# A mixture of experts on one core: norm, routing and first gathers in one stage, job lists from one-hot products, the combine joined to the experts

## The reference, cut to what matters

```python
def hmoe(xn, w_rg, b_rg, w_re, b_re, w_gate, w_up, w_down):
    ...
    lg = (x @ w_rg + b_rg).astype(F32)
    g_sel = jnp.argmax(lg, axis=-1)
    p_g = jnp.max(jax.nn.softmax(lg, axis=-1), axis=-1)
    le = (x @ w_re + b_re).astype(F32).reshape(-1, N_GROUPS, EXPERTS_PER_GROUP)
    le_g = jnp.take_along_axis(le, g_sel[:, None, None], axis=1)[:, 0]
    top_p, top_i = lax.top_k(jax.nn.softmax(le_g, axis=-1), TOP_K_IN_GROUP)
    w_top = p_g[:, None] * top_p / jnp.sum(top_p, axis=-1, keepdims=True)
    ...
        hid = jax.nn.silu(jnp.einsum('nd,edf->nef', x, w_gate[gi])) * jnp.einsum('nd,edf->nef', x, w_up[gi])
        y = y + jnp.einsum('nef,ne,efd->nd', hid, c, w_down[gi]).astype(F32)

def run_group(x, past_len, wkv0, shift0, past_rows, win_buf, P):
    ...
        h = h + y
        h = h + hmoe(rmsnorm(h, P['ln_ffn'][layer]), *moe)
```

## Time and profile before

| | |
|---|---|
| median of 3 runs | 2490.96 us (2485.36 to 2492.52) |
| profiled execution | 2487.45 us, of which span 2485.8 us |
| busy: PE, PEld | 2110.0 us (85%), 1368.9 us (55%) |
| busy: DVE, ACT, POOL | 900.7 us (36%), 487.0 us (20%), 462.1 us (19%) |
| granted TensorE clock, mean | 0.915 |
| bytes moved by DMA | 409.74 MB, mean 165 GB/s |

### The profile page before, as it was taken

One profiled execution on the slowest core, in us unless ns is written; L12 is line 12 of the kernel. 1 busy time (PEld: TensorE's weight loads), 2 busy tenths in 40 slices (PEclk: granted clock), 3 DMA queues, 4 the chain that ended last, 5 costly groups with the idle time before them and its releaser, 6 DMA issues. The chain is left out here.

```text
span 2485.8 us, 44144 instructions
## 1 busy us (share of the span) xinstructions
PE 2110.0 (85%) x17339; PEld 1368.9 (55%) x17339; DVE 900.7 (36%) x1763; ACT 487.0 (20%) x1120; POOL 462.1 (19%) x548
## 2 busy tenths in 40 slices
PE   3899989998953999957987888799999975799993
PEld 2678789994752333326876555455555565233333
DVE  4655247743122111224133666434363022112123
ACT  1311112221011111101001555433343000111100
POOL 0144022220003233320002333000000001323322
PEclk7999999997865999978998999999999895899996
DMA  1498340001252999922440100555547416599952
GB/s 56 144 294 272 113 164 4 6 36 42 68 175 88 374 374 396 373 91 60 112 132 23 32 1 2 177 185 161 184 144 238 148 22 240 215 374 372 394 205 103
DMA packets 238894, 409.74 MB, mean 165 GB/s; under 512 B 56770, under 2 KB 194595, under 8 KB 212436
## 3 DMA queue, kind: packets, MB, share of 16 engines
q1 hardware_dynamic: 191140, 346.48, 38.8%
q0 software_dynamic: 40288, 56.12, 7.3%
q10 hardware_dynamic: 7264, 4.36, 0.6%
HBM read 499.03 MB, written 81.57 MB: 234 GB/s over the span
## 5 line engine op out<-in xcount | busy, mean ns | idle before, releaser
L1619 PE MATMUL banks<-slots,work 128*64 128x512 f32 x1536 | 342.6, 599 | 0.0
L2592 PE MATMUL banks<-slots 128*128 128x508 f32 x512 | 249.2, 601 | 8.7 <-ACT work L2692 7.3
L1619 PEld LDWEIGHTS banks<-slots,work 128*64 128x64 f32 x1536 | 106.2, 138 | 202.7 <-issue 201.8
L909 PE MATMUL banks<-slots 64*64 64x64 f32 x5632 | 188.9, 224 | 23.7 <-issue 7.2
L909 PEld LDWEIGHTS banks<-slots 64*64 64x64 f32 x5632 | 185.1, 140 | 25.8 <-issue 13.9
L671 PE MATMUL banks<-slots,work 128*128 128x260 f32 x768 | 175.3, 387 | 4.6 <-DMA z_state<-in_consts 4.6
L1645 PE MATMUL banks<-slots,work 128*64 128x512 f32 x768 | 175.3, 598 | 3.6 <-DVE work L1697 3.6
L2663 DVE COPY slots<-banks 64x256 f32<-64x256 f32 x256 | 109.2, 426 | 166.8 <-PE banks L2498 162.5
L1891 PE MATMUL banks<-slots,work 128*128 128x260 f32 x640 | 150.0, 397 | 18.0 <-PEq L251 16.2
L671 PEld LDWEIGHTS banks<-slots,work 128*128 128x128 f32 x768 | 145.9, 192 | 32.7 <-issue 6.2
L1331 POOL DMA_INDIRECT expert_lists<-work x20 | 19.6, 981 | 770.0 <-DVEq L251 764.5
(11 more groups left out here) (416 smaller groups left out, 3012.5 us busy)
## 6 DMA issues: line engine op xcount, KB each, us to landing
slots<-in_moe_wgate SPq DMA_DIRECT2D x64, 1024.0 KB, 9.1
slots<-in_moe_wup SPq DMA_DIRECT2D x64, 1024.0 KB, 11.6
slots<-in_moe_wdown SPq DMA_DIRECT2D x64, 1024.0 KB, 11.3
sample_cache_rows<-in_cache_kv POOLq DMA_DIRECT2D x128, 256.0 KB, 4.5
slots<-in_cache_kv SPq DMA_DIRECT2D x256, 128.0 KB, 2.2
slots<-sample_cache_rows SPq DMA_DIRECT2D x32, 512.0 KB, 6.5
slots<-sample_cache_rows SPq DMA_DIRECT2D x64, 256.0 KB, 5.0
slots<-expert_result_rows SPq DMA_DIRECT2D x8, 1024.0 KB, 9.1
```

The costliest lines, as they stand in the source:

```text
L909: last = nc.tensor.matmul(out[half, k, :], block_of(i, u, left)[half, k, :], moving[half, :], start=(x == 0), stop=(x == len(terms) - 1))
L1619: last = mm(c.bank[v][SEAT * j:SEAT * j + SEAT, :], xt[v][:, k, SEAT * j:SEAT * j + SEAT], weights.gate_up_of[2 * s + j][:, k], start=(k = ...
L2592: last = mm(HIDDEN[:, 0:KVH * NCMP_S], s.w1[:, u // NB, j, :], s.xt[u % 2][:, :, j % 8, first:first + NCMP_S], start=(j == 0), stop=(j == 15))
```

## The change

The norm becomes part of the routing stage, so that its loads and the weight loads are issued when the norm begins, and the eight tables become one load. The router's weights become the stationary side: the logits come as 36 rows of 520 columns, the bias is added on VectorE, and five transposes make the token tiles of them. The counts of both kinds come from six matmuls. The lists no longer pass through DRAM: VectorE spreads each entry over 24 columns (which pair) and a one-hot row of 128 (which seat), and ten matmuls add the entries up in PSUM as the lists. The first two fetches stand at the end of this stage. The clears of the fetch buffers move to POOL. The combine becomes the end of the experts stage: SP waits for the scatters, and VectorE makes the sums that POOL made.

```diff
 def route(c, layer, weights):
+    wr = area(KT, NL)
+    both_and_none, place, spill = area(NTILE + 1, E), area(NTILE, E), area(NTILE, E)
+    reached = area(NTILE, PAIRS + 1)
...
         @block.sync
         def _(sp):
+            sp.dma_start(table, io["consts"][:, lo:hi]).then_inc(loaded, 16)
             sp.dma_start(wr[:, :, 0:NG], io["moe_wrg"][layer].rearrange("(k p) n -> p k n", p=P)).then_inc(loaded, 16)
...
-            for dst, name in ((rank4, "rank4"), (rank8, "rank8"), (valid, "valid"), (token, "token"),
-                              (before, "triangle"), (seats, "seats"), (over_id, "overid")):
-                sp.dma_start(dst, io["consts"][:, CCOL[name][0]:CCOL[name][1]]).then_inc(loaded, 16)
...
         @block.gpsimd
         def _(pool):
-            pool.wait_ge(placed, 1)
-            pool.wait_ge(blank_stored, 16)
+            for v in range(2):
+                last = nc.gpsimd.memset(weights.tokens_in[v], 0.0)
+            last.then_inc(cleared, 1)
+            pool.wait_ge(cleared, 1)
+            pool.wait_ge(fetchable, 1)
+            pool.wait_ge(stored, 32)
+            for q in range(2):
+                weights.fetch(q)
+
+        @block.tensor
+        def _(pe):
...
+            pe.wait_ge(loaded, 16 * 5)
+            for k in range(KT):
+                pe.wait_ge(scaled, k + 1)
+                for s in range(2):
+                    last = mm(c.pair[1][0:NL, s, :], wr[:, k, :], x[:, k, span(s)], start=(k == 0), stop=(k == KT - 1))
+            last.then_inc(logits_in, 1)
+            pe.wait_ge(biased, 1)
...
             pe.wait_ge(chosen, 1)
+            mm(c.bank[1][:, 0:E * (NTILE + 1)], before, both_and_none.rearrange("p n e -> p (n e)"), start=True, stop=False)
+            for m in range(NTILE):
+                last = mm(c.bank[1][:, E * (m + 1):E * (NTILE + 1)].rearrange("p (n e) -> p n e", e=E), c.ones,
+                          both[:, m:m + 1, :].to_broadcast([P, NTILE - m, E]), start=False, stop=(m == NTILE - 1))
             last.then_inc(counted, 1)
+            for a in range(2):
+                pe.wait_ge(spread, a + 1)
+                for n in range(NTILE):
+                    last = mm(c.bank[2][:, 0:4 * PAIRS], seat_hot[:, a, n, :], entries[:, a, n].rearrange("p w q -> p (w q)"),
+                              start=(a == 0 and n == 0), stop=(a == 1 and n == NTILE - 1))
+            last.then_inc(listed, 1)
...
         @block.vector
         def _(dve):
+            dve.wait_ge(loaded, 16 * 5)
+            ts(limits, over_id[:, 0:MORE], float(SEAT), float(SEAT), ALU.mult, ALU.add)
+            ts(absent, valid, -FAR, FAR, ALU.mult, ALU.add)
+            dve.wait_ge(summed, 1)
+            ts(halves(root), c.pair[0], 1.0 / D, EPS, ALU.mult, ALU.add).then_inc(means, 1)
...
+            for k in range(KT):
+                nc.vector.scalar_tensor_tensor(x[:, k, :], h[:, k, :], c.vec(f"ffn{layer}", k), rstd, ALU.mult,
+                                               ALU.mult).then_inc(scaled, 1)
+            dve.wait_ge(logits_in, 1)
+            ts(halves(logits_t), c.pair[1][0:NL], bias[0:NL], None, ALU.add).then_inc(biased, 1)
...
+            for a, w in ((0, w1), (1, e2)):
+                tt(both, place, hot[a], ALU.mult)
+                dve.drain()
+                reduce(row[:, a, :].unsqueeze(2), both, AX.X, ALU.add)
+                dve.drain()
+                tt(row[:, a, :], row[:, a, :], absent[:, :, 0], ALU.add)
+                dve.drain()
+                tt(reached, row[:, a, :].unsqueeze(2).to_broadcast([P, NTILE, PAIRS + 1]),
+                   pair_start.unsqueeze(1).to_broadcast([P, NTILE, PAIRS + 1]), ALU.is_ge)
+                dve.drain()
+                reduce(first[:, a, :].unsqueeze(2), reached, AX.X, ALU.add)
+                there = entries[:, a, :, 3, :]
+                tt(there, reached[:, :, 0:PAIRS], reached[:, :, 1:PAIRS + 1], ALU.subtract)
...
+                tt(seat_hot[:, a], lane.unsqueeze(1).to_broadcast([P, NTILE, P]),
+                   seat[:, a, :].unsqueeze(2).to_broadcast([P, NTILE, P]), ALU.is_equal)
+                dve.drain().then_inc(spread, 1)
...
+            dve.wait_ge(listed, 1)
+            out = c.bank[2][:, 0:4 * PAIRS].rearrange("p (w q) -> p w q", w=4)
+            ts(empty, out[:, 3], -FAR, FAR + 0.25, ALU.mult, ALU.add)
+            nc.vector.tensor_copy(c.job_lists[:, :, 2].bitcast(F32), out[:, 2])
+            dve.drain()
+            for w in range(2):
+                tt(c.job_lists[:, :, w], out[:, w], empty, ALU.add)
+            dve.drain().then_inc(fetchable, 1)

 def experts(c, layer, weights):
...
+            sp.wait_ge(finished, PAIRS - 1)
+            for v in range(2):
+                sp.wait_ge(scattered[v], 16 * PAIRS // 2)
+            for n in range(NTILE):
+                m = P if n < TT else NB
+                two = c.expert_rows[2 * P * n:2 * P * n + 2 * m].rearrange("(p a) e -> p a e", a=2)
+                sp.dma_start(pairs[0:m, n], two).then_inc(rows_loaded[n], 16)
...
-            for v in range(2):
-                pool.wait_ge(scattered[v], 16 * PAIRS // 2)
...
+            def sum_rows(n):
+                m = P if n < TT else NB
+                dve.wait_ge(rows_loaded[n], 16)
+                nc.vector.tensor_tensor(pairs[0:m, n, 0, :], pairs[0:m, n, 0, :], pairs[0:m, n, 1, :],
+                                        ALU.add).then_inc(summed, 1)
+
+            sum_rows(0)
             for n in range(NTILE):
...
+                if n + 1 < NTILE:
+                    sum_rows(n + 1)
+                dve.wait_ge(sums_turned, n + 1)
...
 def mixture(c, layer):
-    rms_norm(c, c.slot(0), [(f"ffn{layer}", c.slot(1))], c.slot(3))
     weights = ExpertWeights(c, layer)
     route(c, layer, weights)
     experts(c, layer, weights)
-    combine(c, layer)
```

More of the change, by code:

```diff
@@ L1286, in route @@
     hot = [area(NTILE, E) for _ in range(2)]
-    both, place, spill = area(NTILE, E), area(NTILE, E), area(NTILE, E)
-    valid, token, before = area(NTILE, 1), area(NTILE, 1), area(P)
+    both_and_none, place, spill = area(NTILE + 1, E), area(NTILE, E), area(NTILE, E)
+    both = both_and_none[:, 0:NTILE, :]
     count, jobs_of, start, hop = area(E), area(E), area(E), area(E)
-    ones, seats, over_id = area(E), area(E), area(OVER)
+    ones = area(E)
     limits, past, owner, beyond = area(MORE), area(E, MORE), area(OVER), area(OVER)
@@ L1292, in route @@
     cube = area(OVER, E)
[L1293 to L1298, removed]
+    absent, row, seat, first = area(NTILE, 1), area(2, NTILE), area(2, NTILE), area(2, NTILE)
+    reached = area(NTILE, PAIRS + 1)
+    entries = area(2 * NTILE * 4 * PAIRS).rearrange("p (a n w q) -> p a n w q", a=2, n=NTILE, w=4)
+    seat_hot = c.flat(1, 3)[:, 10560:10560 + 2 * NTILE * P].rearrange("p (a n s) -> p a n s", a=2, n=NTILE)
@@ L1480, in _ @@
                ALU.is_gt)
+            ts(spill, place, float(SEAT), None, ALU.is_ge)
+            tt(place, place, seats.unsqueeze(1).to_broadcast([P, NTILE, E]), ALU.add)
             dve.drain()
@@ new lines, in _ @@
+                there = entries[:, a, :, 3, :]
+                tt(there, reached[:, :, 0:PAIRS], reached[:, :, 1:PAIRS + 1], ALU.subtract)
+                dve.drain()
+                ts(first[:, a, :], first[:, a, :], -float(P), float(P), ALU.mult, ALU.add)
+                tt(entries[:, a, :, 0, :], there, token.to_broadcast([P, NTILE, PAIRS]), ALU.mult)
+                tt(entries[:, a, :, 2, :], there, w.to_broadcast([P, NTILE, PAIRS]), ALU.mult)
+                dve.drain()
+                tt(seat[:, a, :], row[:, a, :], first[:, a, :], ALU.add)
@@ L1648, in _ @@
                 last.then_inc(finished, 1)
+            for n in range(NTILE):
+                m = P if n < TT else NB
+                pe.wait_ge(summed, n + 1)
+                if n >= 2:
+                    pe.wait_ge(added, 2 * (n - 1))
+                for k in range(KT):
+                    last = tr(c.bank[2 * (n % 2) + k // 4][:, P * (k % 4):P * (k % 4) + m],
+                              pairs[0:m, n, 0, P * k:P * k + P], c.ident[0:m, 0:m])
+                last.then_inc(sums_turned, 1)
         @block.scalar
```

243 lines of the change are left out of this document (100 added, 143 removed).

## The result

The changed kernel takes 2391.58 us (median of 4 runs, 2385.08 to 2394.02) against 2491.61 us (median of 4), a ratio of 0.9591 with a 95% interval of 0.9572 to 0.9610. The forecast was 2392. The profiled execution took 2392.51 us, its span 2390.9.

The account below looks back on a forecast made before the run. It took the mixtures' two ends, where one engine works and others wait (some 258 us), as the place to gain: 40.5 + 38.4 + 17.4 = 96.3 from 2487.45 gives 2391.2, forecast 2392 us, range 2381 to 2411.

Parts of the forecast that it names:

- Logits' copy, T0+24.4: Front: logits copied 24.4 us after the squares start (T0), before at T0+48.1; 23.7 us gained in layer 0.
- the two bounds (6.7 and 13.4): Logits' matmuls in the front: 6.7 us at full clock, 13.4 at half clock; 8.9 was taken.
- Copy to first fetch, 29.8: Front: counting and listing put the first token fetch 29.8 us after the logits' copy, bounds 27.5 and 33.
- Stage's end, T0+59.4: Routing stage's end: TensorE turns the first tokens 59.4 us after the squares start; gain 40.5 and 38.4 us.
- two cases: Routing stage's end: TensorE starts at T0+58.6 on the first fetch's landing, or about T0+60.3 if the second's is awaited.
- one of my signs of being wrong: Front: engines wait on POOL for over 4 us between the second fetch and TensorE's first turn of tokens.
- The other three signs: Means wait for a load; logits take over 11 us; combine's loads still start 10 us after the last scatter.
- POOL's end at 0.08 us per DMA: Stage ends: POOL's end grows by about 0.08 us per DMA issued, so two DMAs cost little.
- the rival of a long end at any count: Routing stage's end: POOL's end costs 8.4 us after landing however few its DMAs; 2409 us in all; 12%.
- the rival of the scatter's own completion: Experts' end: the 8.4 us are the scatter's completion, so SP waits as long; 16 us lost, 2408; 8%.
- Tail, 8.7 per layer: Last scatter to next norm: loads start 8.2 us earlier and sums save 0.5, 17.4 us in both layers.
- Sum, 96.3: Total gain: fronts 40.5 and 38.4 us plus tails 17.4, taken from the profiled 2487.45 us.

Follow-up runs that it names:

- the second execution: The changed kernel profiled again without any edit; median 2395.29 us, ratio 0.9608 to the kernel before.
- The two experiments: Changed kernel, one edit each: logits as before with tokens stationary, 2410.64 us; router and expert weight loads issued only once tokens are scaled, 2412.27 us.
- the run without it: Changed kernel with the routing and experts' stages closed without POOL's drain of its DMAs; median 2388.89 us, ratio 0.9597.

## Why the prediction was right, by its steps

**Logits' copy, T0+24.4:** 25.0 and 25.3, and 23.6 twice in the second execution. The matmuls took 9.9 and 10.1 us in the first execution and 8.5 in the second, against 8.9 taken, inside the two bounds (6.7 and 13.4): in layer 0 the granted clock was 0.72 over them in the first and 0.84 in the second. The loads released VectorE 4.0 us after T0, half of what I allowed, without effect. The two experiments give the shares of this step: each of the two edits, taken back alone, returns about 8 us of the 23. The other 7 were not divided further.

**Copy to first fetch, 29.8:** 29.4 and 29.4. Counts came at 13.3, as said. This is the listing without DRAM; its 18 us of gain (47.4 before) stand in the trace and were not tried apart; the place of the fetches ahead of the stage's end was not either.

**Stage's end, T0+59.4:** this was a middle of two cases, and the later was the true one (60.3; measured 60.2 and 60.4). The end waits for the second fetch, 1.5 and 1.6 us by the run without it. By the letter one of my signs of being wrong came up, a wait of over 4 us between second fetch and first turn (4.35 and 4.27); but nearly all of it is that fetch's own landing, which I had priced, and not a long end. The other three signs stayed away.

**POOL's end at 0.08 us per DMA:** taken out, the end gives back 1.63 us at 19 DMAs and 7.9 at 96, and with it in, the way grows at the same price up to 118. The fall beyond that, three readings below 100 could not show. With 2 DMAs it hides under the landing, so the rival of a long end at any count fell, and the rival of the scatter's own completion with it (2.55 us without the end).

**Tail, 8.7 per layer:** 10.3 and 9.4. Loads at 2.2 (2.3 taken) give 8.3 in both layers. The sum on VectorE took 1.23 us (1.25 taken). By the Trainium skill, "VectorE: DVE Perf Modes", section on the TRN2 errata, the estimate was 1.22, and the row agrees. From the first arrival to the end of the last add it took 13.2 and 13.4 (13.4 taken). The term that was off in layer 0 is the first arrival: 4.8 us after the loads' issue, where I kept 6.1. That 6.1 was a reading of layer 0 alone. Timeline of layer 1 in the kernel before:

```profile
2434.69 2.46 SPq L1725 DMA_DIRECT2D slots<-expert_result_rows  x5
2439.48 4.83 POOL L1744 TENSOR_TENSOR slots<-slots 128x1024 f32<-128x1024 f32 x2 [14.28 <-DMA slots<-expert_result_rows]
```

There the first data came 4.79 us after the issue already, so the arrival gives 1.3 us in layer 0 and nothing in layer 1. The two late arrivals on record, 6.07 in the kernel before and 6.37 in the same without POOL's end, are both in layer 0 and go with a longer issue of the five loads (3.23 and 3.54 us); elsewhere the issue takes 2.3 to 2.5 and the data come after 4.7 to 5.1, with the sums on POOL and with combine apart too. Why is open. What is left, from first arrival to next norm, fell by 0.7 us in layer 0 and 1.1 in layer 1, where I took 0.5 for both.

I credited the move of the sums by their speed alone, and by that it is worth 0.8 us. Left on POOL in the joined stage they would cost 7.1 us per layer, because POOL's end then comes behind them.

**Sum, 96.3:** the ways gave 96.8. That the median met the forecast to 0.4 us is partly luck, since unchanged stages move by several us from execution to execution, and the sum starts from an execution that lay 4.2 us below the median of the kernel before (2487.45 and 2491.61): between the medians it is 100.0 us. By experiment 15.7 us of the tails and, for each of two edits alone, some 8 us of each front were taken back, about half of the gain if the two add up. The listing, 18.0 and 17.4 us, is read from rows alone.

## What to carry to other kernels

A stage's end can have an engine that works while all others wait: give the engine that issued many DMAs its last duty early, or let the next work join the stage, and put no work of that engine behind it. Where the stage's own waits already cover those DMAs, as here, where POOL itself waits for the scatters, leaving that end out is the smallest change: one argument gave 15.5 of the 19.7 us of both tails. Read a term in every layer before it goes into a sum: the first arrival was 6.1 us in one layer and 4.8 in the other. Ask of any stage boundary between a fetch and its user which landing it waits for. When runs of one kernel spread as far as the effect, compare the stage's own rows.

## What the runs showed of the hardware

POOL's end of a stage costs about 0.08 us for each DMA that POOL issued in it, beside the landing of the last: 1.63 us at 19 (3.67 with it, 2.04 without), 7.9 at 96 (10.46 and 2.56), and 1.30 more from 102 to 118. At 134 it is down to 4.45 us from the last issue to the next stage's loads.

32 indirect DMAs of 128 rows with 16 bytes each, 64 KB together, beside weight loads brought what the DMA engines move from 424 to 232 GB/s, and the fetch that waits for the token rows' store was issued at T0+64.2 in place of T0+54.5.

Matmuls of 36 columns almost without a pause stayed at 1.2 GHz for 19.5 us, busy 19.32; 32 records of 260 columns at the same place took 9.91 us in one execution and 8.49 in another, the granted clock 0.72 over the first (window above) and 0.84 over the second.
